# Router logits and decay rank by parts of TensorE's columns, with the router's steps in another order

## Chip, cores and metric

One core of a Trainium2 chip runs the whole program. The metric is the device time of one execution in microseconds. The kernel before took 1940.54 us, the median of three runs (1937.41 to 1941.0).

## What is computed

A decoder trunk of two layers on 512 tokens of 1024 channels, all fp32. Each layer adds three blocks to the residual x: a mixer (a convolution in layer 0, gated linear attention, GLA, in layer 1), cross attention to 256 memory tokens, and a mixture of experts. The change touches the router of the experts and the decay of the GLA layer. Cut from the reference:

```
gl = hf @ w_grp + b_grp                     # 4 groups
g_sel = argmax(gl)
el_sel = (hf @ w_exp + b_exp) of group g_sel   # 8 of 32 experts
top_p, top_i = top_k(softmax(el_sel), 2)
gate = softmax(gl)[g_sel] * top_p / sum(top_p)
y = sum over the two experts e of gate * (silu(h @ w_gate[e]) * (h @ w_up[e])) @ w_down[e]

log_a = log_sigmoid(a_lr @ w_a2 + b_a) / 16    # GLA: a_lr = 16 columns of h @ w_in
```

## The kernel before, in words

The program is written by hand as one instruction stream per engine with semaphores between them. TensorE computes, SyncE loads weights into a ring of six 2 MB slots, ScalarE and VectorE take results out of the eight PSUM banks, GpSimd (POOL) adds squares for the norms and issues small loads. x and the normalised h are kept transposed: 8 chunks of 128 channels, each 128 x 512 tokens. An fp32 product is two TensorE instructions.

Output projection of the attention and logits, `xo` on each engine (TensorE L541 to L571). For each chunk c of x, `project_chunk` makes eight products (L430); VectorE's `residual` (L1417) adds the result to x (L1423) and makes h (L1429). Two chunks behind, `follow(c)` (L544) adds the logit product of chunk c, a 36-column stationary `wr` and the 512 tokens of h, into one bank (L549), and turns the chunk to token order by four transposes (L437). ScalarE's `high` (L1182) and VectorE's `low` (L1477) split the turned chunk in a high and a low part, hhi and hlo, for the gather. ScalarE squares x (L1111), POOL adds the squares (L1062). At the end come chunks 6 and 7, the sums of squares by token (`norm_sums`, L395), and the turning of the logits to token order (L568) after ScalarE has copied them (L1191). ScalarE takes the root (`norm_root`, L1121, with a table load), VectorE the reciprocal (L1415).

Router, VectorE's `router(l)` (L1480): scale and bias of the logits (L1508, L1511), maximum and first maximum of the four groups (`first_of`, L1500 to L1503), a penalty for the other groups (L1515, L1517), then the first and the second expert, each by `first_of`. The two masks are added (L1531) and TensorE makes prefix sums over the tokens (L753, L755) and counts by expert (L758), all in one bank. VectorE subtracts the low parts of chunks 6 and 7, makes the table of positions `ptab` (L1538, L1540) and the one-hot of four experts (`make_onehot`, L1588), then the gates (`router_gates`, L1543), which begin by reading the counts (L1556). TensorE waits for all banks to be read (L762) and for the one-hot (L667), gathers the tokens of the first four experts by 64 products (L654), and goes through 16 pairs of experts: `up` for gate and up weights (L601), with two experts of 64 tokens in the two halves of the array's columns, `down` (L616), the scatter (L639) and the next gather.

GLA layer, start (L774 to L803): TensorE projects q and k (L430), then the 16 columns of the decay rank `alr` (L785, recorded at the helper's line L386); VectorE scales it (L1759); TensorE waits for that (L787), projects values, then `z` from `alr` and `wa2` (L798). POOL loads the small matrices `walr` and `wa2` when the experts of layer 0 are done (L1069 to L1073).

## Time and profile before

| | |
|---|---|
| median of three runs | 1940.54 us |
| the profiled execution | 1939.81 us |
| its span on the core | 1938.1 us |
| TensorE busy | 97% of the span |
| VectorE, ScalarE, GpSimd busy | 30%, 19%, 8% |
| mean granted TensorE clock | 0.988 of full |
| HBM traffic | 476.96 MB, mean 246 GB/s |

The span runs from the first to the last record of the core; the execution's time has 1.7 us around it. Busy shares are averages over stages with different limits. Of a timeline row the first two numbers are its start and its length; in square brackets stands how long the engine was idle before it and what ended that. Consecutive matmuls are overlapped in the records, so the length of one (about 0.6 us for 512 columns) is more than what it adds to the stream; busy time divided by count gives that.

### The profile page before, as it was taken

To read this page: it belongs to the slowest core of one execution; us is meant where nothing else is said; L and a number is where in the kernel's file an instruction comes from. 1 tells how busy PE (TensorE), PEld (TensorE's weight loads), DVE (VectorE), ACT (ScalarE), POOL (GpSimd) and SP (SyncE) were. 2 spreads that over 40 slices of the span, in tenths; PEclk is the share of its full clock that TensorE was granted. 3 is DMA by queue.
4 is the path that set the end of the run, shared out by engine and by line. 5 is a ranking of instruction groups with operands and counts; after the bars stand their busy time and mean duration, and the time that the engine had idled before them with its cause. 6 is when DMAs were issued, how large, how long until landed. Compare 5 with 4: busy or idle time off the path is not lost.

```text
span 1938.1 us, 18367 instructions
## 1 busy us (share of the span) xinstructions
PE 1874.7 (97%) x7560; PEld 923.1 (48%) x7560; DVE 584.0 (30%) x1097; ACT 374.2 (19%) x627; POOL 157.3 (8%) x144
## 2 busy tenths in 40 slices
PE   6999999997999999999999999999979999999997
PEld 5445644544444454444443444454444544444443
DVE  3899211223122222222212322213222222222223
ACT  2333211212111111111113232122111111111113
POOL 0566110010000000000020000100100000000001
PEclk9999999998999999999999999999989999999998
DMA  9214422202999999999761211302059999999992
GB/s 360 71 47 169 159 87 87 87 4 87 403 403 409 412 404 414 405 413 408 319 220 44 87 44 44 130 0 90 29 227 403 406 413 405 412 407 415 405 412 101
DMA packets 89771, 476.96 MB, mean 246 GB/s; under 512 B 7614, under 2 KB 8044, under 8 KB 40140
## 3 DMA queue, kind: packets, MB, share of 16 engines
q1 hardware_dynamic: 88636, 470.90, 60.6%
q0 software_dynamic: 496, 2.53, 0.5%
q10 hardware_dynamic: 544, 2.22, 0.3%
q8 instruction: 64, 1.05, 0.2%
q14 instruction: 31, 0.25, 0.0%
HBM read 471.43 MB, written 4.19 MB: 245 GB/s over the span
## 4 chain that ended last, share of the span: by engine, by line
PE 89%; DVE 8%; ACT 1%; issue 1%; DMA 0%; DVEq 0%; SPq 0%; ACTq 0%
PE PS L601 23%; PE PS L430 16%; PE PS L386 13%; PE PS L616 12%; PE PS L639 7%; PE PS L654 7%; DVE PS L1718 5%; PE PS L892 3%; PE PS L525 2%; PE PS L437 1%; PE PS L549 1%; PE PS L646 1%; PE PS L628 1%; PE PS L663 1%; DVE PS L1716 1%
## 5 line engine op out<-in xcount | busy, mean ns | idle before, releaser
L430 PE MATMUL PS<-hT,ring 128*128 128x512 f32 x640 | 277.7, 593 | 4.2 <-issue 3.4
L616 PE MATMUL PS<-ring,hT 128*64 128x512 f32 x1024 | 226.8, 595 | 2.7 <-ACT hT L1217 2.7
L601 PE MATMUL PS<-ring,hT 128*64 128x512 f32 x1024 | 226.3, 595 | 1.3 <-DVE small L1598 1.3
L601 PE MATMUL PS<-ring,xg 128*64 128x512 f32 x1024 | 226.8, 595 | 0.0
L1607 DVE TENSOR_TENSOR xT<-PS,xT 128x512 f32<-128x512 f32 x256 | 159.3, 682 | 212.7 <-PE PS L639 212.6
L430 PEld LDWEIGHTS PS<-hT,ring 128*128 128x128 f32 x640 | 120.8, 190 | 152.2 <-issue 151.1
L601 PEld LDWEIGHTS PS<-ring,hT 128*64 128x64 f32 x1024 | 73.8, 137 | 133.1 <-issue 131.4
L601 PEld LDWEIGHTS PS<-ring,xg 128*64 128x64 f32 x1024 | 72.2, 137 | 132.6 <-issue 132.4
L616 PEld LDWEIGHTS PS<-ring,hT 128*64 128x64 f32 x1024 | 70.7, 137 | 135.1 <-issue 127.9
L1633 DVE TENSOR_TENSOR ylo<-PS,yhi 128x1024 fp32r<-128x1024 f32 x32 | 39.2, 1224 | 301.6 <-ACT yhi L1222 301.6
L639 PE MATMUL PS<-onehotT,yhi 128*128 128x512 f32 x256 | 116.0, 453 | 3.6 <-DVE ylo L1633 3.6
L386 PE MATMUL PS<-ring,hT 128*128 128x512 f32 x256 | 111.9, 594 | 0.8 <-DVE RK L1759 0.8
L1718 DVE SCALAR_TENSOR_TENSOR PS<-RU,R,PS 128x512 f32<-128x512 f32 x168 | 111.3, 747 | 0.0
L639 PE MATMUL PS<-onehotT,ylo 128*128 128x512 f32 x256 | 103.0, 402 | 0.0
L1062 POOL TENSOR_TENSOR dg<-memT 128x512 f32<-128x512 f32 x6 | 7.6, 1274 | 1076.8 <-ACT memT L1111 1076.8
L654 PE MATMUL PS<-onehot,hhi 128*128 128x256 f32 x512 | 89.3, 298 | 4.6 <-DVE small L1556 2.3
L1628 DVE SCALAR_TENSOR_TENSOR hT<-hT,small,PS 128x512 f32<-128x512 f32 x32 | 23.9, 747 | 212.6 <-PE PS L601 212.6
L639 PEld LDWEIGHTS PS<-onehotT,yhi 128*128 128x128 f32 x256 | 49.0, 191 | 81.7 <-issue 48.7
L1217 ACT ACTIVATE hT<-PS 128x512 f32<-128x512 f32 x32 | 19.2, 599 | 355.6 <-PE PS L646 355.6
L654 PEld LDWEIGHTS PS<-onehot,hhi 128*128 128x128 f32 x512 | 72.5, 198 | 27.5 <-issue 27.5
L430 PE MATMUL PS<-RC,ring 128*128 128x512 f32 x192 | 84.4, 592 | 0.0
L654 PE MATMUL PS<-onehot,hlo 128*128 128x256 f32 x512 | 84.3, 288 | 0.0
(259 smaller groups left out, 1767.3 us busy)
## 6 DMA issues: line engine op xcount, KB each, us to landing
ring<-in_moe_w_gate SPq DMA_DIRECT2D x128, 1024.0 KB, 11.4
ring<-in_moe_w_up SPq DMA_DIRECT2D x128, 1024.0 KB, 12.2
ring<-in_moe_w_down SPq DMA_DIRECT2D x128, 1024.0 KB, 9.2
ring<-in_xa_w_kv SPq DMA_DIRECT2D x16, 1024.0 KB, 7.5
ring<-in_gla_w_in SPq DMA_DIRECT2D x12, 1024.0 KB, 13.0
ring<-in_conv_w_in SPq DMA_DIRECT2D x8, 1024.0 KB, 14.4
ring<-in_xa_w_q SPq DMA_DIRECT2D x8, 1024.0 KB, 6.7
ring<-in_xa_w_o SPq DMA_DIRECT2D x8, 1024.0 KB, 6.9
```

What stands on the lines that cost most here:

```text
L386: mm = pe.matmul(o, lhs(k), rhs(k), start=(k == 0), stop=(k == nk - 1))
L430: mm = pe.matmul(bank(b), w[:, k * 512 + m * P:k * 512 + (m + 1) * P], src[:, k, :], start=(k == 0), stop=(k == C - 1))
L525: mm = pe.matmul(bank(b), w[:, k * 512 + m * P:k * 512 + (m + 1) * P], oT[:, k, :], start=(k == 0), stop=(k == C - 1))
L601: mm = pe.matmul(PS[e * SL:(e + 1) * SL, kind * BANK:(kind + 1) * BANK], x[:, k, (2 * (p % 2) + e) * SL:(2 * (p % 2) + e + 1) * SL], ring[ ...
L616: mm = pe.matmul(PS[e * SL:(e + 1) * SL, (2 + half) * BANK:(3 + half) * BANK], hidT[:, k, e * SL:(e + 1) * SL], ring[:, pair_slot(l, 4 + e ...
L639: mm = pe.matmul(bank(b), w[:, c * P:(c + 1) * P], onehotT[:, :], start=(w is yhi), stop=(w is ylo))
L654: mm = pe.matmul(bank(b, (c - c0) * 256, (c - c0 + 1) * 256), h[:, t, c * P:(c + 1) * P], onehot[:, q % 2, t, :], start=(h is hhi and t == 0),
L892: mm = pe.matmul(bank(b), w[:, k * 512 + (m % 4) * P:k * 512 + (m % 4 + 1) * P], goT[k], start=(k == 0), stop=(k == C - 1))
L1607: dve.tensor_tensor(xT[:, c, :], bank(XBANK + b), xT[:, c, :], ALU.add).then_inc(g[f"x_read{b}"], 1)
L1628: dve.scalar_tensor_tensor(hidden, sil, gcol, bank(1), ALU.mult, ALU.mult).then_inc(g["hidden_ready"], 1)
L1633: dve.tensor_tensor(ylo[:, :], PS[:, 2 * BANK:4 * BANK], yhi[:, :].bitcast(F32), ALU.subtract).then_inc(g["ylo_done"], 1)
L1718: ins = dve.scalar_tensor_tensor(acc, src, w, acc, ALU.mult, ALU.add)
```

## The change

- Logits: `wr` is widened to 64 columns, the new ones zero. Chunks are taken in pairs, the even one into partitions 0 to 63 of the bank (column half 0), the odd one into 64 to 127. The turn of the logits becomes a product with `fold`, two identities one below the other, which also adds the halves. Pairs (0,1), (2,3), (4,5) follow the projections 3, 5 and 7; pair (6,7) comes ahead of the turns of chunks 6 and 7, the latter behind the logits' turn.
- ScalarE copies the logits ahead of `high(6)`, and takes a root of a constant at the start of `xo`, so that the table is loaded there.
- VectorE: `low(6)` ahead of the norm's reciprocal; scale and bias in one operation for each of four token tiles; the penalty folded into the masking of the logits; each mask is its own fp32r tile. TensorE makes the prefix sums of the first mask when it is there and adds those of the second; the counts get eight products and bank 4 to themselves, and their reading is waited for only after the first gather.
- Positions count from 1 (so does the iota), which drops the subtraction (L1540). The first one-hot is made in four operations, one for each tile of 128 tokens, and the first products of the opening gather wait for them one by one.
- Decay rank: the 8 chunks' products go to four column quarters (32 columns each, 16 of them zero), two rounds; `alr` has 128 partitions and `wa2` holds four copies, at 32-row steps, with zero rows between, so that `z` adds the quarters. POOL clears both and issues five loads instead of two.

The diff, without tile sizes repeated elsewhere:

```diff
+HOTS = NQ + TT - 1
...
-            ptab = sb("ptab", [P, NQ, TT * QUAD], where=s)
+            ptab = sb("ptab", [P, TT, NE], where=s)
...
-                wr = sb("wr", [P, C, NG + NE], where=before)
+                wr = sb("wr", [P, C, SL], where=before)
...
-                mkR = sb("mkR", [P, TT, NE], F32R, where=before)
-                rt = sb("rt", [P, 660], where=before)
+                hotR = [sb(f"hotR{j}", [P, TT, NE], F32R, where=before) for j in range(2)]
+                rt = sb("rt", [P, 532], where=before)
...
-        walr = RU[:, C * T:C * T + C * RANK].rearrange("p (c r) -> p c r", c=C)
-        wa2 = RC[0:RANK, 7 * T:8 * T]
-        alr = RK[0:RANK, 7 * T:8 * T]
+        walr = AT[:, 0:2, :].rearrange("p a (c r) -> p (a c) r", r=32)
+        wa2 = RC[:, 7 * T:8 * T]
+        alr = RK[:, 7 * T:8 * T]
...
+        fold = small[:, 152:152 + NG + NE]
...
 
-                def follow(c):
-                    wait_h(pe, ni, c)
-                    if c == 0:
+                def logits(c0):
+                    if c0 == 0:
                         take(("lg", l), LOGIT_BANK)
                         pe.wait_ge(s_wr, 64 * (l + 1))
-                    mm = pe.matmul(PS[0:NG + NE, LOGIT_BANK * BANK:(LOGIT_BANK + 1) * BANK], wr[:, c, :], hT[:, c, :],
-                                   start=(c == 0), stop=(c == C - 1))
-                    if c == C - 1:
+                        pe.wait_ge(wr_pad, l + 1)
+                    for c in (c0, c0 + 1):
+                        wait_h(pe, ni, c)
+                    for c in (c0, c0 + 1):
+                        o = SL * (c % 2)
+                        mm = pe.matmul(PS[o:o + SL, LOGIT_BANK * BANK:(LOGIT_BANK + 1) * BANK], wr[:, c, :], hT[:, c, :],
+                                       start=(c0 == 0), stop=(c0 == C - 2))
+                    if c0 == C - 2:
                         mm.then_inc(bank_full[LOGIT_BANK], 1)
+
+                def turn_h(c):
+                    wait_h(pe, ni, c)
                     transposes(("ht", l, c), [hT[:, c, t * P:(t + 1) * P] for t in range(TT)])
 
                 for i in range(2):
@@ -558,16 +570,20 @@
                     for m in range(2 - 2 * i, 4):
                         c = 4 * i + m
                         project_chunk(w, m, ("xo", l, c), oT)
-                        follow(c - 2)
-                follow(C - 2)
-                follow(C - 1)
+                        turn_h(c - 2)
+                        if c % 2:
+                            logits(c - 3)
+                logits(C - 2)
+                turn_h(C - 2)
                 norm_sums(ni)
                 b = take(("lt", l))
+                pe.wait_ge(s_const, 2)
                 pe.wait_ge(lgT_ready, l + 1)
                 for t in range(TT):
-                    mm = pe.transpose(bank(b, t * (NG + NE), (t + 1) * (NG + NE)), lgT[0:NG + NE, t * P:(t + 1) * P],
-                                      ident[0:NG + NE, 0:NG + NE])
+                    mm = pe.matmul(bank(b, t * (NG + NE), (t + 1) * (NG + NE)), lgT[:, t * P:(t + 1) * P], fold,
+                                   start=True, stop=True)
                 mm.then_inc(bank_full[b], 1)
+                turn_h(C - 1)
                 plan.width = 8
...
-                def gather(q, p, k, c0):
+                def gather(q, p, k, c0, opening=False):
                     b, done = use(p, k)
                     for c in (c0, c0 + 1):
                         for h in (hhi, hlo):
                             for t in range(TT):
+                                if opening and c == c0 and h is hhi:
+                                    pe.wait_ge(g["onehot_ready"], HOTS * r + t + 1)
                                 mm = pe.matmul(bank(b, (c - c0) * 256, (c - c0 + 1) * 256), h[:, t, c * P:(c + 1) * P],
                                                onehot[:, q % 2, t, :], start=(h is hhi and t == 0),
...
-                pe.wait_ge(g["onehot_ready"], NQ * r + 1)
                 for i in range(4):
-                    gather(0, -1, 8 + i, 2 * i)
+                    gather(0, -1, 8 + i, 2 * i, i == 0)
+                if main:
+                    pe.wait_ge(*read(("ct", l)))
...
-                pe.wait_ge(mask_ready, l + 1)
-                mk = mkR[:, :, :].rearrange("p t e -> p (t e)")
-                pe.matmul(bank(b, 0, TT * NE), triR[:, :], mk, start=True, stop=False, skip_group_check=True)
-                for t in range(1, TT):
-                    pe.matmul(bank(b, t * NE, TT * NE), onesR[:, :], mk[:, 0:(TT - t) * NE], start=False,
-                              stop=(t == TT - 1), skip_group_check=True)
+                for j in range(2):
+                    pe.wait_ge(hot_ready[j], l + 1)
+                    mk = hotR[j][:, :, :].rearrange("p t e -> p (t e)")
+                    pe.matmul(bank(b, 0, TT * NE), triR[:, :], mk, start=(j == 0), stop=False, skip_group_check=True)
+                    for t in range(1, TT):
+                        mm = pe.matmul(bank(b, t * NE, TT * NE), onesR[:, :], mk[:, 0:(TT - t) * NE], start=False,
+                                       stop=(j == 1 and t == TT - 1), skip_group_check=True)
+                mm.then_inc(bank_full[b], 1)
+                b = take(("ct", l), 4)
                 for t in range(TT):
-                    mm = pe.matmul(bank(b, TT * NE, (TT + 1) * NE), onesR[:, :], mkR[:, t, :], start=(t == 0),
-                                   stop=(t == TT - 1), skip_group_check=True)
+                    for j in range(2):
+                        mm = pe.matmul(bank(b, 0, NE), onesR[:, :], hotR[j][:, t, :], start=(t == 0 and j == 0),
+                                       stop=(t == TT - 1 and j == 1))
                 mm.then_inc(bank_full[b], 1)
+                own = plan.at[("ct", l)][0]
                 for b in range(8):
-                    pe.wait_ge(bank_read[b], plan.uses[b])
+                    if b != own:
+                        pe.wait_ge(bank_read[b], plan.uses[b])
...
-            pe.wait_ge(s_gld, 32)
+            pe.wait_ge(s_gld, 80)
             b = take(("alr",))
-            group(PS[0:RANK, b * BANK:(b + 1) * BANK], lambda k: walr[:, k, :], lambda k: hT[:, k, :],
-                  C).then_inc(bank_full[b], 1)
+            for k in range(C):
+                o = 32 * (k % 4)
+                mm = pe.matmul(PS[o:o + 32, b * BANK:(b + 1) * BANK], walr[:, k, :], hT[:, k, :], start=(k < 4),
+                               stop=(k >= 4))
+            mm.then_inc(bank_full[b], 1)
...
+                    pool.memset(walr, 0.0).then_inc(low_pad, 1)
+                    pool.memset(wa2, 0.0).then_inc(low_pad, 1)
+                    pool.wait_ge(low_pad, 2)
                     with nc.allow_non_contiguous_dma(reason="16 columns of a wide matrix"):
-                        pool.dma_start(walr, a["gla_w_in"][0][:, 2048:2048 + RANK].rearrange("(k p) n -> p k n", p=P)
+                        pool.dma_start(walr[:, :, 0:RANK], a["gla_w_in"][0][:, 2048:2048 + RANK].rearrange("(k p) n -> p k n", p=P)
                                        ).then_inc(s_gld, 16)
-                    pool.dma_start(wa2, a["gla_w_a2"][0]).then_inc(s_gld, 16)
+                    for j in range(4):
+                        pool.dma_start(wa2[32 * j:32 * j + RANK, :], a["gla_w_a2"][0]).then_inc(s_gld, 16)
...
+                pool.memset(wr[:, :, NG + NE:], 0.0).then_inc(wr_pad, 1)
...
+                act.activation(small[:, 150:151], ones[:, 0:1], ACT.Sqrt)
                 for c in range(C):
                     square(ni, c)
                     if c >= 2:
                         high(c - 2)
-                high(C - 2)
                 act.wait_ge(*full(("lg", l)))
-                act.activation(lgT[0:NG + NE, :], PS[0:NG + NE, LOGIT_BANK * BANK:(LOGIT_BANK + 1) * BANK], ACT.Copy
-                               ).then_inc(bank_read[LOGIT_BANK], 1)
+                act.activation(lgT[:, :], bank(LOGIT_BANK), ACT.Copy).then_inc(bank_read[LOGIT_BANK], 1)
                 act.wait_ge(*read(("lg", l)))
                 act.sem_inc(lgT_ready, 1)
+                high(C - 2)
                 norm_root(ni)
                 high(C - 1)
...
+                low(l, C - 2)
                 norm_recip(3 + 3 * l)
                 dve.wait_ge(*full(("lt", l)))
                 b = plan.at[("lt", l)][0]
-                dve.tensor_tensor(lg[:, :, :], bank(b, 0, TT * W).rearrange("p (t w) -> p t w", t=TT),
-                                  rrec.unsqueeze(2).to_broadcast([P, TT, W]), ALU.mult).then_inc(bank_read[b], 1)
+                for t in range(TT):
+                    ins = dve.scalar_tensor_tensor(lg[:, t, :], bank(b, t * W, (t + 1) * W), rrec[:, t:t + 1], bt[:, :],
+                                                   ALU.mult, ALU.add)
+                ins.then_inc(bank_read[b], 1)
                 dve.wait_ge(*read(("lt", l)))
-                link(dve.tensor_tensor(lg[:, :, :], lg[:, :, :], bt[:, :].unsqueeze(1).to_broadcast([P, TT, W]), ALU.add))
                 link(dve.tensor_reduce(mx, gl, AX.X, ALU.max))
                 dve.tensor_tensor(gin, gl, wide(mx, NG), ALU.subtract).then_inc(rin_ready, 1)
-                link(first_of(gl, mx, NG, ohg))
-                link(dve.tensor_scalar(pen, ohg, BIG, -BIG, ALU.mult, ALU.add))
+                link(first_of(gl, mx, NG, off, ALU.not_equal))
                 for t in range(TT):
-                    ins = dve.tensor_tensor(elm[:, t, :].rearrange("p (g e) -> p g e", g=NG),
-                                            lg[:, t, NG:W].rearrange("p (g e) -> p g e", g=NG),
-                                            pen[:, t, :].unsqueeze(2).to_broadcast([P, NG, EG]), ALU.add)
-                    if t < TT - 1:
-                        ins.then_inc(dve_chain, 1)
-                        chain[0] += 1
-                    else:
-                        link(ins)
+                    dve.scalar_tensor_tensor(elm[:, t, :].rearrange("p (g e) -> p g e", g=NG),
+                                             off[:, t, :].unsqueeze(2).to_broadcast([P, NG, EG]), -BIG,
+                                             lg[:, t, NG:W].rearrange("p (g e) -> p g e", g=NG), ALU.mult,
+                                             ALU.add).then_inc(elm_ready, 1)
+                dve.wait_ge(elm_ready, TT * (l + 1))
                 link(dve.tensor_reduce(mx, elm, AX.X, ALU.max))
-                link(first_of(elm, mx, NE, hot1))
+                first_of(elm, mx, NE, hotR[0][:, :, :]).then_inc(hot_ready[0], 1)
+                dve.wait_ge(hot_ready[0], l + 1)
                 link(dve.scalar_tensor_tensor(elm, hot1, -2.0 * BIG, elm, ALU.mult, ALU.add))
                 link(dve.tensor_reduce(m2, elm, AX.X, ALU.max))
                 dve.tensor_tensor(din, m2, mx, ALU.subtract).then_inc(rin_ready, 1)
-                link(first_of(elm, m2, NE, hot2))
-                dve.tensor_tensor(mkR[:, :, :], hot1, hot2, ALU.add).then_inc(mask_ready, 1)
-
-                low(l, C - 2)
+                first_of(elm, m2, NE, hotR[1][:, :, :]).then_inc(hot_ready[1], 1)
+                dve.wait_ge(hot_ready[1], l + 1)
+                link(dve.tensor_tensor(mask, hot1, hot2, ALU.add))
                 low(l, C - 1)
                 dve.wait_ge(*full(("cs", l)))
                 b = plan.at[("cs", l)][0]
-                mask = mkR[:, :, :].bitcast(F32)
-                link(dve.scalar_tensor_tensor(eq, bank(b, 0, TT * NE).rearrange("p (t e) -> p t e", t=TT), 1.0, mask,
-                                              ALU.add, ALU.mult))
-                link(dve.tensor_scalar(ptab[:, :, :].rearrange("p q (t e) -> p q t e", e=QUAD),
-                                       eq.rearrange("p t (q e) -> p q t e", e=QUAD), -1.0, None, ALU.add))
+                dve.scalar_tensor_tensor(ptab[:, :, :], bank(b, 0, TT * NE).rearrange("p (t e) -> p t e", t=TT), 1.0,
+                                         mask, ALU.add, ALU.mult).then_inc(bank_read[b], 1)
+                dve.wait_ge(*read(("cs", l)))
...
-                b = plan.at[("cs", l)][0]
-                dve.tensor_reduce(maxc, bank(b, TT * NE, (TT + 1) * NE), AX.X, ALU.max).then_inc(bank_read[b], 1)
+                dve.wait_ge(*full(("ct", l)))
+                b = plan.at[("ct", l)][0]
+                dve.tensor_reduce(maxc, bank(b, 0, NE), AX.X, ALU.max).then_inc(bank_read[b], 1)
...
-                    tab = ptab[:, q, :].unsqueeze(2).to_broadcast([P, TT * QUAD, SL])
-                    hot = onehot[:, q % 2, :, :].rearrange("p t (e s) -> p (t e) s", e=QUAD)
-                    dve.tensor_tensor(hot, iota[:, :].unsqueeze(1).to_broadcast([P, TT * QUAD, SL]), tab,
-                                      ALU.is_equal).then_inc(g["onehot_ready"], 1)
+                    n = 1 if q == 0 else TT
+                    for t in range(0, TT, n):
+                        tab = ptab[:, t:t + n, q * QUAD:(q + 1) * QUAD].unsqueeze(3).to_broadcast([P, n, QUAD, SL])
+                        hot = onehot[:, q % 2, t:t + n, :].rearrange("p t (e s) -> p t e s", e=QUAD)
+                        dve.tensor_tensor(hot, iota[:, :].unsqueeze(1).unsqueeze(1).to_broadcast([P, n, QUAD, SL]),
+                                          tab, ALU.is_equal).then_inc(g["onehot_ready"], 1)
```

## Rows read from the trace of the kernel before

**Rows 1.** The page, busy time, share of the span and instructions

```profile
PE 1874.7 (97%) x7560; PEld 923.1 (48%) x7560; DVE 584.0 (30%) x1097; ACT 374.2 (19%) x627; POOL 157.3 (8%) x144
```

**Rows 2.** Groups by shape: count | busy us, mean ns | idle before them

```profile
L430 PE MATMUL PS<-hT,ring 128*128 128x512 f32 x640 | 277.7, 593 | 4.2 <-issue 3.4 <-DVE hT L1684 0.8
...
L601 PE MATMUL PS<-ring,xg 128*64 128x512 f32 x1024 | 226.8, 595 | 0.0
...
L549 PE MATMUL PS<-hT,wr 128*36 128x512 f32 x32 | 16.8, 606 | 0.0
```

**Rows 3.** Waits of TensorE: us in total, times, longest

```profile
PE PS L753 <- DVE mkR L1531: 14.6, 2, 7.3
```

**Rows 4.** Waits of SyncE's queue

```profile
SPq L962 <- PE PS L601: 476.2, 120, 30.4
```

**Rows 5.** Timeline of layer 0, end of the output projection: start, us, engine

```profile
443.22 1.05 PE L549 MATMUL PS<-hT,wr 128*36 128x512 f32 x2
...
444.20 0.66 PE L437 MATMUL PS<-ident,hT 128*128 128x128 f32 x4
...
444.69 7.03 PE L430 MATMUL PS<-RC,ring 128*128 128x512 f32 x16
...
451.65 1.05 PE L549 MATMUL PS<-hT,wr 128*36 128x512 f32 x2
...
452.49 0.48 DVE L1429 TENSOR_SCALAR hT<-xT,vecT 128x512 f32<-128x512 f32 x1
...
453.20 1.27 POOL L1062 TENSOR_TENSOR dg<-memT,dg 128x512 f32<-128x512 f32 x1 [7.17 <-ACT memT L1111]
...
453.96 0.69 DVE L1477 TENSOR_TENSOR hlo<-PS,hhi 128x512 fp32r<-128x512 f32 x1 [0.98 <-ACT hhi L1182]
...
456.26 0.95 PE L395 MATMUL PS<-ones,dg 128*128 128x1 f32 x8
456.56 1.28 ACT L1121 ACT_TABLE_LOAD   x1
...
457.14 0.43 PE L568 MATMUL PS<-ident,lgT 36*128 36x36 f32 x4
...
458.28 0.31 DVE L1508 TENSOR_TENSOR lg<-PS,small 128x144 f32<-128x144 f32 x1
```

**Rows 6.** The same timeline, router chain to the first gather

```profile
460.08 0.17 DVE L1515 TENSOR_SCALAR rt<-rt 128x16 f32<-128x16 f32 x1
460.29 0.50 DVE L1517 TENSOR_TENSOR rt<-lg,rt 128x32 f32<-128x32 f32 x4
...
464.45 0.29 DVE L1531 TENSOR_TENSOR mkR<-rt 128x128 fp32r<-128x128 f32 x1
...
464.89 0.45 PE L753 MATMUL PS<-mkR,triR 128*128 128x128 f32 x1 [7.31 <-DVE mkR L1531]
...
465.73 1.01 PE L758 MATMUL PS<-mkR,onesR 128*128 128x32 f32 x4
466.79 0.29 DVE L1538 SCALAR_TENSOR_TENSOR rt<-PS,mkR 128x128 f32<-128x128 f32 x1 [0.85 <-PE PS L758]
...
467.37 1.23 DVE L1588 TENSOR_TENSOR onehot<-iota,ptab 128x1024 fp32r<-128x1024 f32 x1
...
469.09 1.20 PE L654 MATMUL PS<-onehot,hhi 128*128 128x256 f32 x4 [2.34 <-DVE small L1556]
```

**Rows 7.** Timeline of layer 1's start: a small load, the decay products

```profile
980.89 0.51 POOL L1073 DMA_DIRECT2D RC<-in_gla_w_a  x1
...
1031.54 7.04 PE L386 MATMUL PS<-hT,RU 128*16 128x512 f32 x16
...
1038.62 0.68 DVE L1759 TENSOR_TENSOR RK<-PS,memT 16x512 f32<-16x512 f32 x1 [6.28 <-PE PS L386]
```

**Rows 8.** Windows: stretch, busy by engine, granted clock, DMA

```profile
460.50:461.00 0.50, 0.00 (x0) 0.00 (x0) 0.47 (x4) 0.00 (x0) 0.00 (x0) 0.90 0.89 377
...
474.50:475.00 0.50, 0.50 (x6) 0.50 (x5) 0.00 (x0) 0.00 (x0) 0.00 (x0) 0.95 0.00 0
```

47 lines of the change are left out of this document (26 added, 21 removed).

## The prediction

> **What bounds the kernel now.** I read the page first. TensorE is busy for 97% of the span [rows 1], so a change pays where it shortens TensorE's stream or its waits. Grouped by shape, one full-width fp32 instruction of 512 columns costs 277.7 / 640 = 0.434 us of stream, and one that uses 64 columns of the array costs 226.8 / 1024 = 0.2215 us [rows 2]: the two halves of a pair run side by side. The logits have 36 columns and use whole-width time: 32 instructions, two to a product [rows 2]. The table of waits gives the second place: TensorE's largest waits are the two before the prefix sums of the router masks, 14.6 us together, both of the same length [rows 3]. The same view of SyncE's queue says that the weight loads wait for TensorE, not it for them [rows 4], so time won at a router or in the GLA layer should stay won: the expert stage behind it goes at TensorE's pace.
>
> The timeline then shows the first router; the second repeats it. Inside the output projection each logit product costs 444.20 - 443.22 = 0.98 us, turning a chunk 0.49, then 16 projection instructions follow [rows 5]. The projection ends at 451.65, which I call E. From E to VectorE's first router operation at 458.28 are 6.63 us: three logit products, three turns, norm sums (456.26) and logit turn (457.14). ScalarE's table load of 1.28 us (from 456.56) stands ahead of the root from which that operation's reciprocal is taken [rows 5]. From there VectorE's chain takes 6.61 us to TensorE's first prefix product at 464.89, and 4.20 more pass until the first gather at 469.09 [rows 6].
>
> **The change, part by part, for one router.**
>
> A, ahead of E: five single logit steps become two pair steps. A pair is four half-width instructions, 4 x 0.2215 = 0.89, and the same 0.11 of switching (0.98 less 2 x 0.434) gives 1.00. Saved: 5 x 0.98 - 2 x 1.00 = 2.90 us. All of it is TensorE's own stream; the weights lie in SBUF long before.
>
> B, from E to VectorE's first operation: one turn (0.60 with the switch), two pair steps, one turn (0.49), norm sums (457.14 - 456.26 = 0.88). Chunk 7 of h is ready at 452.49 + 0.49, 1.33 after E, before the last pair asks for it at 1.6. The last square sum on POOL ends at 453.20 + 1.27, 2.82 after E, before the norm sums at 3.1 [rows 5]. The logit turn becomes a real product with a folding matrix: eight fp32 instructions with full loads, where four stood in 0.43; the nearest row is the norm sums, also eight, so 0.88 and a tenth until they can be read. Total 0.60 + 2.00 + 0.49 + 0.88 + 0.98 = 5.0 against 6.63, saved 1.6. Beside it ScalarE copies the logits from 2.8 to 3.4 (before the fold at 4.0), and takes the root by 4.3, since the table load now comes before the squares, where ScalarE waits for the residual. Were that cover gone, 1.28 would come back. The moved subtraction of h's low part (0.69 on VectorE [rows 5]) ends at about 4.7 and the reciprocal at 4.9, just inside 5.0: this is what comes next if the fold is cheaper. The turn of chunk 7 goes behind the fold, under VectorE's chain.
>
> C, VectorE's chain: four operations of the kind of the four masks (0.50 together) replace two of 0.31 in sequence, saving 0.12; the penalty operation goes, 0.21; the mask addition leaves the way to the sums, 464.89 - 464.45 less its wait, 0.33 [rows 5, 6]. Saved 0.66. The sums of the first choice run under the search for the second.
>
> D, from the second choice to the first gather: now four prefix products (465.73 - 464.89 = 0.84), then eight count products instead of four at 1.01 / 4 = 0.25, together 2.84. Beside that, VectorE adds the mask, subtracts chunk 7 (0.69), waits for the prefix sums at 1.0, makes the table in 0.32 and the first quarter of the one-hot: 1.23 / 4 is 0.31 and a quarter alone cannot exceed 1.23; with a fixed part, 0.43. It is ready by 1.9, and each further tile by 0.35 more, so the count sums bind at 2.84 against 4.20: saved 1.36. The whole of 1.23 could cost at most 0.3 more than this for the first tile. The other tables (gates, counts) follow on VectorE as before and are used only behind the 64 gather products, which cover them.
>
> A to D: 2.90 + 1.63 + 0.66 + 1.36 = 6.55, twice 13.1 us.
>
> E2, decay rank: sixteen full-width instructions from 1031.54, read at 1038.62: 7.08 us, with TensorE waiting on the eviction afterwards, as it still will [rows 7]. No row has quarters. Bounds: no overlap, nothing saved; overlap as of halves, 16 x 0.2215 + 0.17 = 3.7, saved 3.4; four abreast, two rounds of 0.886 + 0.17 = 1.9, saved 5.1. Halves overlap without loss, so I take 5.1. Eviction on 128 instead of 16 partitions, and products over 128 instead of 16 rows, stream the same 512 columns. POOL gets two memsets and three more issues of some 0.51 us ahead of its spill reload; it starts at 980 and the sums are due at 1031 [rows 7]. Even 10 us are hidden; without that cover they would be TensorE's idle time. The router's memset (224 columns) stands ahead of four small loads, which no product waits for now; the first logits come one chunk, some 8 us, later than before, which covers it.
>
> Here rows and the Trainium skill differ. The rows give halves the full factor of two (0.434 / 0.2215 = 1.96). "TensorE: Matmul & The Clock Gate", section "Measured speedup vs the span model", measured only 2.38x for three column tiles, 79% of the ideal. At 79% the same sum would be about 16.1 instead of 18.2, a time near 1923.7.
>
> **Sum.** 13.1 + 5.1 = 18.2. The profiled execution took 1939.81, 1.7 over its span and 0.7 under the median of the runs, so 1921.6 us.
>
> The clock: TensorE's granted clock falls from 2.4 to 1.2 GHz at 460.9 (a mean of 0.90 over the half microsecond), 3.3 us after its last product, and returns at 474.55 (0.95), 5.5 us after gathering began [rows 8]. After the change the idle stretch to the first choice's sums is still about 3.4 us (E + 5.5 to E + 8.9), and another of one follows. I leave the loss as it is; where the fall and the return lie may differ by 1 us a router either way.
>
> **Rivals.**
> 1. Quarters gain no more than halves. For: full use of the array by four streams appears nowhere in the trace. Against: two streams cost nothing. 1921.6 + 1.7 = 1923.3. Chance 0.11.
> 2. The clock never falls, since sums of the first choice break the gap of 7.3 us. Saves half of 5.5, and about 0.9 of the count sums, per router: 7.2, so 1914.4. Against: 3.3 us were enough for the fall. Chance 0.07.
> 3. The parts don't run side by side, so the change doesn't do what it says: a pair costs 4 x 0.434 + 0.11 = 1.85. A and B shrink by 4 x 0.85 per router and E2 goes: 18.2 - 6.8 - 5.1 = 6.3 saved, 1933.5. Against: the half-width rows. Chance 0.04.
> 4. Slower: in the logits and decay products every change of column group exposes the weight load (0.14) and the tail of the instruction before (0.606 - 0.434 = 0.17). Place: 32 logit and 16 decay instructions; price 48 x 0.31 = 14.9 on top of rival 3, so 1948.4. It turns the change into a loss from 6.3 / 48 = 0.13 us per instruction on. For: the narrow steps change groups with every product, and are short. Against: experts do the same for 2048 instructions without it. Chance 0.03.
>
> **How the numbers follow.** Forecast 0.75, rivals 0.11, 0.07, 0.04, 0.03. About 0.2% (3.9 us) is what a measurement can tell from no change: faster 0.96, same 0.01, slower 0.03. Range: the clock's 2 us and the runs' own spread (1937.4 to 1941.0) about 1921.6, drawn out to rival 1 above and part of rival 2 below: 1916.5 to 1926.0. Rivals 3 and 4 and the full value of 2 stay out, 0.14 with a few strays.
>
> **What would show it.** Right: logit instructions on 64 columns at about 0.22 us each, E some 2.9 earlier; VectorE's first router operation 5.0 after E; first gather 2.8 after the second choice's prefix product, released by no one-hot; decay products about 1.9 us to their eviction; nothing else moved, expert periods the same. Wrong: a table load before the root, TensorE idle before the last pair or before the fold, gathers waiting on tiles, decay instructions at 0.22 or 0.43 each, or granted clock at full through the router.

## The result and the profile after

| | before | changed |
|---|---|---|
| median of the timed runs, us | 1941.0 (1937.4 to 1948.4, 5 runs) | 1920.23 (1917.7 to 1926.2, 5 runs) |
| ratio, 95% interval | | 0.9896 (0.9877 to 0.9915) |
| profiled execution, us | 1939.81 | 1920.17 |
| its span, mean granted clock | 1938.1, 0.988 | 1918.0, 0.990 |

The change is faster by 20.8 us, with 1921.6 forecast. Six more executions of the same kernel on another occasion gave 1922.07; the eleven together have a median of 1921.65.

The page of the changed kernel, to set beside [rows 1]:

```profile
span 1918.0 us, 18457 instructions
PE 1864.5 (97%) x7584; PEld 924.7 (48%) x7584; DVE 583.6 (30%) x1104; ACT 373.6 (19%) x629; POOL 159.9 (8%) x151
```

Its groups by shape (columns as in [rows 2]) show the logits, the new fold and the decay products:

```profile
L558 PE MATMUL PS<-hT,wr 128*64 128x512 f32 x32 | 8.5, 616 | 0.0
L583 PE MATMUL PS<-small,lgT 128*128 128x36 f32 x16 | 2.1, 279 | 0.0
L812 PE MATMUL PS<-hT,AT 128*32 128x512 f32 x16 | 1.9, 598 | 0.0
```

A single logit instruction is no shorter than before (616 ns from its start to its end, against 606), but 32 of them now fill 8.5 us of stream. The sixteen decay instructions fill 1.9, each as long by itself as a full one. What overlaps is seen in the group's busy time, never in the mean of one.

TensorE's waits, against [rows 3]:

```profile
PE PS L773 <- DVE hotR L1536: 9.4, 4, 3.8
PE PS L442 <- ACT hT L1149: 6.3, 1, 6.3
```

The waits ahead of the prefix sums were 14.6 us in two pieces of 7.3; now they are 9.4 in four, none over 3.8. The second line is near the end of the program, at 1903.7 of 1918.0 us, before the outputs are turned; it was 5.4 before. It returns below.

The timeline of layer 0, from the projection of chunk 2 (of 0 to 7) through the router, with the columns of [rows 5]:

```profile
402.65 7.03 PE L435 MATMUL PS<-RC,ring 128*128 128x512 f32 x16
...
416.82 0.60 PE L442 MATMUL PS<-ident,hT 128*128 128x128 f32 x4
417.35 1.08 PE L558 MATMUL PS<-hT,wr 128*64 128x512 f32 x4
418.36 7.13 PE L435 MATMUL PS<-RC,ring 128*128 128x512 f32 x16
425.33 0.60 PE L442 MATMUL PS<-ident,hT 128*128 128x128 f32 x4
...
448.45 0.60 PE L442 MATMUL PS<-ident,hT 128*128 128x128 f32 x4
448.98 2.11 PE L558 MATMUL PS<-hT,wr 128*64 128x512 f32 x8
...
451.52 1.00 PE L400 MATMUL PS<-ones,dg 128*128 128x1 f32 x8
452.38 1.06 PE L583 MATMUL PS<-small,lgT 128*128 128x36 f32 x8
453.08 0.17 DVE L1448 RECIPROCAL small<-small 128x4 f32<-128x4 f32 x1
453.28 0.63 PE L442 MATMUL PS<-ident,hT 128*128 128x128 f32 x4
453.55 0.74 DVE L1543 SCALAR_TENSOR_TENSOR lg<-PS,small,bt 128x36 f32<-128x36 f32 x4 [0.30 <-PE PS L583]
454.32 0.17 DVE L1547 TENSOR_REDUCE rt<-lg 128x4 f32<-128x16 f32 x1
...
457.71 0.45 PE L773 MATMUL PS<-hotR,triR 128*128 128x128 f32 x1 [3.80 <-DVE hotR L1536]
459.63 0.47 PE L773 MATMUL PS<-hotR,triR 128*128 128x128 f32 x1 [0.92 <-DVE hotR L1536]
460.51 1.87 PE L781 MATMUL PS<-hotR,onesR 128*128 128x32 f32 x8
461.03 1.43 DVE L1621 TENSOR_TENSOR onehot<-iota,ptab 128x256 fp32r<-128x256 f32 x4
462.21 1.20 PE L672 MATMUL PS<-onehot,hhi 128*128 128x256 f32 x4
...
472.28 7.95 PE L617 MATMUL PS<-ring,hT 128*64 128x512 f32 x36 [0.65 <-DVE small L1631]
```

E, the end of the output projection, lies at 448.45. VectorE's first router operation starts 5.10 later, waiting for the fold alone (the reciprocal ends 0.30 before). The last prefix product starts at 459.63, the first gather at 462.21 without a wait, the experts at 472.28. The gap of 7.3 us is broken by the first choice's sums at 457.71.

The same timeline at the start of layer 1, against [rows 7]:

```profile
1024.08 1.92 PE L812 MATMUL PS<-hT,AT 128*32 128x512 f32 x16
1026.07 0.69 DVE L1793 TENSOR_TENSOR RK<-PS,memT 128x512 f32<-128x512 f32 x1 [1.19 <-PE PS L812]
1026.82 7.13 PE L391 MATMUL PS<-ring,hT 128*128 128x512 f32 x16 [0.81 <-DVE RK L1793]
```

From the first decay product to the eviction are 1.99 us, where 7.08 were. Nothing waits for the extra copies of the weights.

Windows over the clock, against [rows 8], at its fall and its return:

```profile
454.00:455.00 1.00, 0.00 (x0) 0.00 (x0) 0.90 (x6) 0.98 (x2) 0.00 (x0) 0.90 1.00 426
465.00:465.50 0.50, 0.50 (x6) 0.50 (x6) 0.47 (x5) 0.00 (x0) 0.00 (x0) 0.95 0.00 0
```

The mean of 0.90 over the first microsecond puts the fall of the granted clock at 454.8, 0.9 us after the last product of 453.28 has ended, and the 0.95 puts its return at 465.05, 2.8 us after the first gather; before, it fell 3.3 us after the last product and came back 5.5 us into the gathers.

**Where the 20 us come from.** The table splits the profiled executions by stage; layers 0 and 1 are given with a slash where they differ by more than 0.05. "Gather to experts" is from the first gather to the first expert product.

| stage, us | before | changed | saved per router |
|---|---|---|---|
| start of chunk 2's projection to E | 49.14 | 45.80 | 3.34 |
| E to first router operation | 6.63 | 5.10 | 1.53 |
| to last prefix product | 6.61 | 6.08 | 0.53 |
| to first gather | 4.20/4.12 | 2.58 | 1.6 |
| gather to experts | 11.25/11.57 | 10.07 | 1.2/1.5 |
| decay products to eviction (layer 1) | 7.08 | 1.99 | 5.09, once |

The experts of layer 0 start 8.06 us sooner (480.34 to 472.28), those of layer 1 21.35 (1428.91 to 1407.56). Of the 13.29 between, 5.1 are the decay stage and 8.4 the second router; 0.2 are lost elsewhere. Behind the start of layer 1's experts 1.2 are given back: near the end of the program the wait before the output turn grows from 5.37 to 6.28, and TensorE stands at half clock there. The span is 20.1 shorter.

### The profile page after: what moved, and what is told of

Its sections match the earlier page's. It is cut to its first block, busy times and chain, and to the rows that moved or that the text cites. A ratio compares the mean times of both kernels' runs of the same rounds, so it can differ in the third digit from the quotient of the medians.

```text
span 1918.0 us, 18457 instructions
## 1 busy us (share of the span) xinstructions
PE 1864.5 (97%) x7584; PEld 924.7 (48%) x7584; DVE 583.6 (30%) x1104; ACT 373.6 (19%) x629; POOL 159.9 (8%) x151
## 4 chain that ended last, share of the span: by engine, by line
PE 90%; DVE 7%; ACT 1%; issue 1%; DMA 0%; SPq 0%; DVEq 0%; ACTq 0%
PE PS L617 23%; PE PS L435 17%; PE PS L391 13%; PE PS L632 12%; PE PS L655 7%; PE PS L672 7%; DVE PS L1752 5%; PE PS L920 3%; PE PS L530 2%; PE PS L442 1%; PE PS L662 1%; PE PS L644 1%; PE PS L681 1%; DVE PS L1750 1%; PE PS L875 0%
## 6 DMA issues: line engine op xcount, KB each, us to landing
ring<-in_moe_w_gate SPq DMA_DIRECT2D x128, 1024.0 KB, 11.2
```

## The experiments

**The decay products: four abreast, two, or none.** One kernel puts all eight chunks into one column group, the other alternates between two.

```diff
-                o = 32 * (k % 4)          # changed: start=(k < 4), stop=(k >= 4)
+                o = 0                     # whole: start=(k == 0), stop=(k == C - 1); eviction and product on 32 rows
+                o = 64 * (k % 2)          # halves: start=(k < 2), stop=(k >= C - 2)
```

> The changed kernel with the eight decay products all in one column group of 32, one behind the other; the rest as changed. My theory (four quarters run abreast): start of the products to VectorE's eviction goes from 1.99 us back to 7.1 us, the start of the next projection product from 2.74 to 7.8 us behind the first decay product, and the whole program is 5.1 us longer, give or take the clock. Rival (the gain came from the smaller stationary or the load, not from running abreast): the sixteen instructions stay near 0.12 us each and nothing is lost.

> The decay products in two column groups (32 columns at 0 and at 64) instead of four, in four rounds. My theory: time goes by rounds, one round being as long as one full-width product (0.87 us), so the products take 4 x 0.87 + 0.17 = 3.7 us to the eviction, 1.7 us more than with four groups. Rival (two groups already bring the most there is): 2.0 us as with four, no difference. Second rival (the price is per instruction, 0.12 us): also 2.0 us.

The timeline of the first kernel, then of the second:

```profile
1023.64 7.05 PE L811 MATMUL PS<-hT,AT 128*32 128x512 f32 x16
1030.73 0.68 DVE L1792 TENSOR_TENSOR RK<-PS,memT 32x512 f32<-32x512 f32 x1 [6.29 <-PE PS L811]
```

```profile
1027.29 3.63 PE L812 MATMUL PS<-hT,AT 128*32 128x512 f32 x16
1030.97 0.69 DVE L1793 TENSOR_TENSOR RK<-PS,memT 128x512 f32<-128x512 f32 x1 [2.88 <-PE PS L812]
```

To the eviction: 7.09 in one group, 3.68 in two, 1.99 in four. Less the 0.17 of tail behind the last stream these are 6.92, 3.51 and 1.82, so two groups divide the stream by 1.97 and four by 3.80. The times were 1925.25 and 1924.16, one run each. Quarters gain almost all that they could over halves, so rival 1 falls; the eviction costs 0.7 whatever its rows. By the 79% of the Trainium skill ("TensorE: Matmul & The Clock Gate", section "Measured speedup vs the span model") my estimate would be about 2.4; this chip showed 1.99 for this shape.

**The logits without halves.** Both chunks of a pair go to the same 64 columns; the copy and the fold then need 64 rows instead of 128, order and all else stay.

```diff
-                        o = SL * (c % 2)
-                                       start=(c0 == 0), stop=(c0 == C - 2))
+                        o = 0
+                                       start=(c == 0), stop=(c == C - 1))
```

> The changed kernel with both chunks of each logit pair in column half 0, so that they run one behind the other; order, fold and everything else as changed. My theory (A and B came from the halves running side by side): each of the four pair steps grows from 1.0 to 1.85 us, so the end of the projection comes 1.7 us later and VectorE's first router operation another 1.7 us later behind it, 3.4 us a router, 6.8 us in all. Rival (the gain came from pairing the steps, with fewer switches between projection, logits and turns): a pair grows by less than 0.3 us. Second rival (the later start is hidden by the norm sums' own chain): the second half of the 3.4 us does not show.

```profile
451.96 0.60 PE L442 MATMUL PS<-ident,hT 128*128 128x128 f32 x4
452.49 3.65 PE L557 MATMUL PS<-hT,wr 128*64 128x512 f32 x8
458.63 0.74 DVE L1542 SCALAR_TENSOR_TENSOR lg<-PS,small,bt 128x36 f32<-128x36 f32 x4 [0.34 <-PE PS L582]
```

Eight instructions take 3.65 instead of 2.11. The output projection takes 47.51 (45.80 changed, 49.14 before), and E to the first router operation 6.67. So in B the halves are the whole gain (6.67 against 6.63 before): one product more (four after E, three before) and the longer fold use up what the early table and the later turn of chunk 7 bring. Ahead of E the halves bring 1.71, and the other 1.63 come from one product fewer before E (four, where five were) and from fewer and cheaper switches. It ran in 1927.62, 6.0 over 1921.65; the two routers' 2 x (1.71 + 1.57) are 6.6.

**The tail of the router: one-hot by tiles, counts.** In one kernel the first one-hot is built whole again. In another VectorE writes the sum of both choices as one mask, and four count products do instead of eight.

```diff
-                    n = 1 if q == 0 else TT      # one-hot whole
+                    n = TT
-                    for j in range(2):           # counts once
-                        mm = pe.matmul(bank(b, 0, NE), onesR[:, :], hotR[j][:, t, :], ...)
+                    mm = pe.matmul(bank(b, 0, NE), onesR[:, :], maskR[:, t, :], start=(t == 0), stop=(t == TT - 1))
```

> The changed kernel with the first one-hot made in one operation of 1024 columns and one wait in front of the opening gather. My theory (the eight count products set the gather's start, the one-hot is ready about then): the first gather starts 0.1 to 0.3 us later behind the second choice's prefix product, 2.6 becomes 2.7 to 2.9 us, under 0.6 us in all, less than the clock's variation. Rival (the tiles are what let the gather start early): it starts 0.9 us later or more, at over 3.4 us.

> The changed kernel with the added mask kept as an fp32r tile and the counts made from it, by four products instead of eight. My theory (the eight count products stand between the one-hot and the gather): the gather starts when the first one-hot tile is ready, 1.9 to 2.0 us behind the second choice's prefix product instead of 2.58, 0.6 us a router. Rival (the gather is set by the one-hot tiles or by the chain on VectorE): still 2.5 to 2.6 us.

The timeline of the kernel with the whole one-hot:

```profile
462.27 1.87 PE L781 MATMUL PS<-hotR,onesR 128*128 128x32 f32 x8
462.79 1.23 DVE L1621 TENSOR_TENSOR onehot<-iota,ptab 128x1024 fp32r<-128x1024 f32 x1
464.16 1.19 PE L672 MATMUL PS<-onehot,hhi 128*128 128x256 f32 x4
```

The gather starts 2.77 after the last prefix product instead of 2.58, so the tiles are worth 0.19 a router while eight count products stand in the way. That of the kernel that counts once:

```profile
457.48 0.48 PE L775 MATMUL PS<-hotR,triR 128*128 128x128 f32 x1 [0.92 <-DVE hotR L1537]
458.35 1.01 PE L783 MATMUL PS<-maskR,onesR 128*128 128x32 f32 x4
458.88 1.43 DVE L1624 TENSOR_TENSOR onehot<-iota,ptab 128x256 fp32r<-128x256 f32 x4
459.45 0.83 PE L674 MATMUL PS<-onehot,hhi 128*128 128x256 f32 x2
```

Now the first tile binds, and the gather comes 1.97 after the prefix product: 0.61 a router, 1.2 in all. But the gather then takes 10.64/10.62 instead of 10.07/10.08, since 3.7 us of it run at half clock instead of 2.8 and its first products wait for the tiles. From the last prefix product to the experts it is 12.62/12.59 against 12.65/12.67, so in these two profiles almost nothing is left of the 0.61. Yet the one look gave 1914.53, seven less than the changed kernel. Such a surplus has to be found or distrusted, so the same kernel was timed:

> The kernel of e4 (counts once, no filled gaps), timed. By the stages it should be 1.2 us faster than the changed kernel's 1920.2, so 1919.0; the single 1914.5 seen before had its clock at full at two other places where the changed kernel's profile shows a spell at half, worth some 3.4 us, and should come out as a lucky one. Rival (the 1914.5 is what the kernel does): a median of 1916 or less.

It gave 1923.02 (1918.3 to 1925.2, six runs), ratio 0.9904 (0.9887 to 0.9921), with the stage again at 1.97. So the 1914.5 was a lucky look, and of the 1.2 expected nothing shows (1919.0 was the forecast). The lucky look had no spell of half clock in two stretches where the changed kernel and the kernel before have one (mean granted clock 1.00 against 0.96 in 960 to 1000 us and in 1300 to 1340), each worth 40 x 0.04 = 1.6. Its span is 5.6 shorter than the changed kernel's: 3.4 of it lie between the two routers, where these stretches are, 2.2 ahead of the output projection of layer 0, where the code is the same, and 0.1 at the two routers together. The six timed runs had mean clocks of 0.987 to 0.991. The 0.61 a router is shown by the one stage; as a time of the program it is not shown.

**The early load of ScalarE's table**, taken out of the changed kernel, and put alone into the kernel before:

```diff
-                act.activation(small[:, 150:151], ones[:, 0:1], ACT.Sqrt)
```

> The changed kernel without the root of a constant at the start of the output projection's ScalarE part, so the table is loaded when the root is due. My theory: ScalarE is free at 4.0 us behind the end of the projection, the load of 1.28 then stands on the way, the root ends at 5.4 and VectorE's first router operation starts at 5.8 instead of 5.10 us, 0.7 us a router. Rival (the fold on TensorE binds, with room for the load): no change, 5.10 us. Second rival (the whole load shows): 6.4 us.

> The kernel before with one thing of the change alone: the root of a constant ahead of the squares, so that ScalarE's table is loaded early. My theory (before, the load stood on the way between norm sums and reciprocal): VectorE's first router operation comes 6.0 us behind the end of the projection instead of 6.63, held then by the norm sums and the logit turn on TensorE; 0.6 us a router, 1.2 in all. Rival (the turn on TensorE bound it already): 6.6 us as before.

The timeline of the changed kernel without it:

```profile
452.80 1.28 ACT L1154 ACT_TABLE_LOAD   x1
454.30 0.18 DVE L1447 RECIPROCAL small<-small 128x4 f32<-128x4 f32 x1 [0.79 <-ACT small L1154]
```

The reciprocal waits for the root, and the first router operation comes 5.72 after E instead of 5.10. In the kernel before, the early load brings 6.63 to 6.03. So it is worth 0.62 and 0.60 a router. The rest of the 1.28 was hidden: in the kernel before under the norm sums (the load starts at 456.56, the sums end only at 457.2), in the changed kernel under VectorE's `low(6)` and the fold, which hold the reciprocal and the first operation anyway. The two ran in 1923.77 and 1941.89 (1941.0 for the kernel before beside it): the second, by this stage 1.2 faster, came out 0.9 slower. Its gather to the experts took 10.08/10.13, where the same code took 11.25/11.57 in the kernel before. So its two routers are 3.8 shorter, and the rest of its span is 5.9 longer in code that is the same: 2.2 ahead of the projection, 2.4 between the routers, where its clock is at half for a stretch that the kernel before doesn't have (a mean of 0.66 from 1050 to 1060 us), and 1.3 at the end. One look can't resolve 1.2 us.

**The clock.** Does TensorE's idle time make the gather slow, and is it worth filling? Three kernels add products whose results nobody reads, of the normed h against ones. The first puts four of 512 columns behind the turn of the last chunk and one of 384 between the choices; the second adds the single count to that; the third widens the product between the choices to 512 columns and puts one more of 512 before the counts.

```diff
+                for c in range(4):                     # after the last turn
+                    pe.matmul(bank(LOGIT_BANK), ones[:, :], hT[:, c, :], start=True, stop=True)
+                    if j:                              # between the choices; third kernel: 512
+                        pe.matmul(bank(LOGIT_BANK, 0, 384), ones[:, :], hT[:, 0, 0:384], start=True, stop=True)
+                pe.matmul(bank(LOGIT_BANK), ones[:, :], hT[:, 1, :], start=True, stop=True)  # third, before the counts
```

> The changed kernel with products into an unused bank in TensorE's two idle stretches of the router: four full fp32 products behind the last turn, one of 384 columns between the two choices; their results are not read. My theory (the idle stretch of 3.8 us makes the clock fall, and half of the router's gather runs at 1.2 GHz for it): the granted clock stays at full, the prefix and count products take half the time, so that the gather starts at 1.9 to 2.0 us instead of 2.58, and from the gather's start to the first expert product are 8.5 us instead of 10 to 11.5; together 2.2 to 3.5 us a router, 5.7 us in all, so about 1915. Rival (the clock falls anyway, or the added products hold up the first choice's sums): no gain, or up to 1 us lost per router.

> The two foregoing together. If the clock stays at full, the eight count products take only 1 us and are no longer in the way, so counting once adds nothing beyond the filled gaps: gather at 1.9 to 2.0 us, the same time within 0.3 us. If the clock falls all the same, it gains 0.6 us a router over the changed kernel and no more.

> The kernel of e9 with a full 512-column fp32 product between the choices (instead of 384 columns) and another one between the prefix products of the second choice and the counts, where TensorE waits for the one-hot anyway. In e6 and e9 the clock still fell, 0.5 us into the counts and at the gather's start. My theory (short products behind waits do not hold the clock, long ones do): it now stays at full through the gather; gather still at 1.8 us behind the second choice's prefix, 8.5 us from the gather to the first expert product where e9 had 10.4 and 10.6; 4 us less than e9 in all, about 1916 to 1917. Rival (the added product delays the counts and the gather): gather at over 2.2 us. Second rival (the clock falls all the same): 10 us or more, and no gain over e9.

Windows of the first, around the first gather:

```profile
460.00:460.50 0.50, 0.50 (x7) 0.50 (x6) 0.50 (x1) 0.00 (x0) 0.00 (x0) 0.97 0.32 131
460.50:461.00 0.50, 0.50 (x5) 0.50 (x4) 0.47 (x3) 0.00 (x0) 0.00 (x0) 0.50 0.00 0
```

Though the long gap was filled, the clock fell at 460.5, in the middle of the row of count products, with TensorE busy throughout both windows (since 459.59, after 0.59 us idle, and 0.37 us idle at 457.3); it stayed at half until 467.3. The gather to the experts took 11.61 us. The stage before it was quicker (1.81, since the prefix sums and the first count products ran at full clock), so the loss had only moved. The second kernel had it at half from 463.2 to 466.7, where it fell in a wait of 0.73 us for the first tile, and took 10.38.

Windows of the third, then its timeline:

```profile
462.00:464.00 2.00, 2.00 (x11) 1.38 (x10) 1.92 (x8) 0.00 (x0) 0.00 (x0) 1.00 0.00 0
464.00:466.00 2.00, 2.00 (x20) 2.00 (x18) 1.74 (x9) 0.51 (x1) 0.00 (x0) 1.00 0.04 8
```

```profile
461.42 1.11 PE L784 MATMUL PS<-hT,ones 128*128 128x512 f32 x2
462.18 1.43 DVE L1629 TENSOR_TENSOR onehot<-iota,ptab 128x256 fp32r<-128x256 f32 x4
462.75 1.30 PE L676 MATMUL PS<-onehot,hhi 128*128 128x256 f32 x4
463.88 0.64 PE L676 MATMUL PS<-onehot,hlo 128*128 128x256 f32 x4
```

Here the clock is full throughout, and the gather takes 9.4 us instead of 10.0 to 11.5 (8.5 was expected). Its first four products stand 1.13 us on the one-hot tiles, which arrive every 0.35; at the 0.118 us that a gather product takes at full clock they would need 0.5.

| | gather to experts | time, runs | ratio, 95% |
|---|---|---|---|
| changed | 10.07 to 11.34 | 1921.65, 11 | 0.9896, 0.9904 |
| gap filled | 11.61/10.92 | 1919.43, 4 | 0.9888 (0.9865 to 0.9911) |
| and counts once | 10.38/10.56 | 1920.82, 4 | 0.9895 (0.9876 to 0.9914) |
| and wider | 9.38/9.40 | 1917.78, 4 | 0.9880 (0.9858 to 0.9901) |

The last has the lowest median, but its interval overlaps that of the changed kernel, and the two weren't timed on one chip together. The kernel that only counts once was: on the same chip it gave 1923.02 in six runs with mean clocks of 0.987 to 0.991, where the wide fills gave 1917.78 in four with 0.993 to 0.996. So the fills do raise the clock, and the 5.2 us less are a hint that they pay; their intervals still overlap, and no version was shown to beat the change.

**The changed kernel once more**, to see what its own time scatters by:

> The changed kernel itself, timed again, with a second profile. My theory (what differs from run to run is where the clock's spells at half fall): every stage that is not products at the clock's mercy repeats to 0.02 us: 5.10 from the end of the projection to VectorE's first router operation, 6.08 to the second choice's prefix products, 2.58 to the gather, 1.99 for the decay products; from the gather to the first expert product anything from 10.0 to 11.5 us. The median comes out between 1918 and 1923, and runs with a lower mean clock take longer. Rival (the first five runs were fast by the chip or by luck, the change is worth 16 us or less): a median over 1925.

1922.07 (1919.4 to 1926.7, six runs), ratio 0.9904 (0.9887 to 0.9921). Every stage before the gather agrees within 0.02 with the first profile; the gather to the experts took 11.34/10.42 instead of 10.07/10.08. The windows of that stage (columns as in [rows 8]) show why, first layer 0 of the first profile, then layers 0 and 1 of the second:

```profile
462.21:472.28 10.07, 9.42 (x69) 9.36 (x70) 4.86 (x24) 2.72 (x5) 0.00 (x0) 0.86 0.01 2
```

```profile
464.72:476.06 11.34, 10.69 (x69) 10.63 (x70) 4.85 (x24) 2.71 (x5) 0.00 (x0) 0.75 0.01 1
1398.62:1409.04 10.42, 9.77 (x70) 9.71 (x70) 4.85 (x24) 2.71 (x5) 0.00 (x0) 0.83 0.00 0
```

A mean clock of 0.86 over 10.07 us is 2.8 us at half; 0.75 and 0.83 are 5.7 and 3.6. The same holds for the kernel before (0.76 and 0.74, 5.5 and 6.1 us at half, 11.25 and 11.57) and for it with the early table (0.86 and 0.85, 2.9 us, 10.08 and 10.13). So this stage's length goes with how much of it runs at half clock, in the same way in both kernels: a microsecond more at half costs a little under 0.5.

The times follow the clock: the runs with mean clocks of 0.990, 0.989 and 0.986 took 1919.4, 1921.7 and 1926.5. Not all scatter lies in the router: chunk 2's projection starts at 405.17 in the second profile, 2.5 us later than in the first, by the same code.

## Why the prediction was right

The forecast was 1921.6, the median 1920.23; the saving 18.2 forecast, 19.6 between the two profiled executions. The stages bear it out one by one; that the median of the eleven runs, 1921.65, meets the forecast to the tenth is luck, with single runs between 1917.7 and 1926.7.

- **A**, 2.90 forecast, 3.34 measured. A pair cost 1.01, as said (1.00). Under-sized was the rest: a projection with no logit product next to it takes 6.87 us to the next instruction's start instead of 6.97, four times (the two that come straight behind a pair still take 6.97), and a turn directly behind it 0.43 instead of 0.49, three times, against 0.53 where a pair follows the turn, twice. The halves are 1.71 of it, by the kernel without them.
- **B**, 1.63 forecast, 1.53 measured: 5.10 against 5.0. The chain was the one named (fold last, reciprocal 0.30 ahead), and the cover that the early table gives is worth 0.62, where the text put all of the 1.28 at stake.
- **C**, 0.66 forecast, 0.53 measured. The mis-sized term: four operations "of the kind of the four masks (0.50 together)" took 0.77 to the next one's start, and the two that they replace had taken 0.68 by the same measure, so the 0.12 of gain was a loss of 0.09. These four read PSUM and the masks don't, which may be why; no run separates it. The removals of the penalty and of the mask addition gave 0.08 more than their 0.54.
- **D**, 1.36 forecast, 1.6 measured. The count sums bound, as said, but took 1.70 from their start to the gather's (460.51 to 462.21) instead of 2.0; the tile was ready in time, and wins only 0.19 over the whole one-hot.
- **Decay rank**, 5.1 forecast, 5.09 measured, by two rounds of a full instruction. Halves took 3.68 (forecast 3.7). Rival 1 is refuted. Rivals 3 and 4 too: no column group exposed a load or a tail.
- **The clock**, left as it was, within 1 us a router: it gained 1.2 and 1.5 in the profiled pair. Read by itself that would be a gain of the change; but the same instructions of the gather took 10.0 to 11.5 in the changed kernel and in five others which differ from it elsewhere or in the stages before, in the repeat of the changed kernel 1.3 more in layer 0, and in the kernel before with the early table 1.2 and 1.4 less than in the kernel before. How much of the stage ran at half accounts for it (2.8 us in the changed kernel, 5.5 and 6.1 before, 2.9 before with the early table), so it is scatter between executions, on which the change has no shown hold. **Rival 2** didn't come: breaking the gap of 7.3 us into 3.8 and 0.9 left the fall in place, and even earlier. What a full clock would bring is shown by the one profile of the kernel with wide products in every gap: from the last prefix product of layer 0 to its experts 1.80 + 9.38 = 11.2 us, against 12.6 and 13.4 in the two profiles that only count once. So a full clock is worth 1.4 to 2.3 a router here. The rival's 3.6 rested on gathers that stand at half for 5.5 us, as in the kernel before; where only 2.8 to 5.7 us were at half there was less to win, and waiting for the tiles takes back another 0.6.
- **The end.** 1.2 us come back, with a wait of 6.28 instead of 5.37 before the last output turn, at half clock. The text named no cost there, and rightly: it isn't the change's. The kernel before with the early table has the long wait too (its timeline row stands below), and three variants of the changed kernel (table late, decay in halves, wide fills) have the short one, 5.3. In each of this case's profiles with the short wait, and in no other, a short spell at half clock lies some 20 to 24 us before the end. Why that shortens the wait stays open.

```profile
1925.85 3.65 PE L437 MATMUL PS<-ident,hT 128*128 128x128 f32 x16 [6.28 <-ACT hT L1116]
```

Together: 6.55 forecast for A to D, 7.0 measured; twice 0.45, and 2.7 of the clock's scatter, less 1.2 at the end and 0.4 spread over the rest of the two layers, lead from 18.2 to 20.2, where the span shows 20.1; the profiled times differ by 19.64, since 1.7 and 2.2 us lie around the two spans.

## What to carry to other kernels

Where a product has few output columns and its reduction splits over chunks, put the chunks into column groups side by side: 7.1 us became 3.7 and 2.0, for the price of replicated weights and of a fold. The fold is free where a product with the partial sums must follow anyway (`z`: its eight instructions from start to the next one took 3.4 us, 3.6 before), and costs about 0.5 us where it replaces four short transposes (0.90 from the fold's start to the turn behind it, where the transposes took 0.43). Cost such a chain stage by stage against its own rows: A to D came to 7.0 a router with 6.55 forecast. Don't read a gain of a few microseconds in one profile as the change's before the same stage has been seen in a second execution: here the clock moved a single stage by 1.5 us with the same code. And count what is won ahead of a stretch at half clock only behind that stretch: of 0.61 us won before the gather less than 0.1 was left at the experts, in the one pair of profiles that shows it.

## What the hardware showed that was not expected

- Four column groups of 32 run abreast nearly without loss (3.80 for 4), with eight chunks in two rounds; 0.31 us of switching per instruction, which rival 4 asked about, appears nowhere.
- Filling the long gap didn't keep the clock up. In the kernel with the filled gap it fell to 1.2 GHz amid count products, when TensorE had been busy for 0.9 us and idle for only 0.59 and 0.37 before that. It stayed at 2.4 GHz through both routers in the one profile with 512-column products in every gap; that kernel also has shorter idle stretches (0.38 and 0.36), and no run separates the two.
- In layer 0 the fall came 0.9 us after TensorE's last product in the changed kernel, 0.3 in its second profile (455.79 + 0.64 to 456.74), and 3.3 in the kernel before, so an idle stretch can't be priced by its length alone.
- VectorE took 0.185 us for an operation of 36 columns from PSUM in a chain of four, against 0.125 for the mask operations of the same chain.
